# Attention of a streaming encoder layer: when the streams' loads are asked for, how many splits precede the first job, and in what rounds the value products run

## The reference, cut to what matters

```
z = rmsnorm(x) @ w_in                      # q_A k_A v_A forget_A q_B k_B v_B
A (8 heads x 64): softmax(q k^T / 8 + C[t] - C[s]), s <= t, C = cumsum(log sigmoid(f))
B (8 heads x 64): softmax(q k^T / 8 + rel_bias[t-s]), own chunk of 64 and the 8 before it
streams: the same, with 1024 cached keys (A) or 512 (B) before the 16 new ones
x += rmsnorm(concat(rmsnorm(o_A), rmsnorm(o_B)) @ w_out)
x += rmsnorm((silu(h @ w_gate) * (h @ w_up)) @ w_down)
```

## Time and profile before

| what | us |
|---|---|
| median of 3 runs (lowest, highest) | 3291.67 (3288.47, 3296.19) |
| the profiled execution's own time | 3288.23 |
| its span, first to last instruction | 3286.5 |
| TensorE busy over the span | 2942.9 (90%) |
| VectorE, ScalarE, GpSimd busy | 1659.4, 1208.5, 469.6 |

### The profile page before, as it was taken

How to read it: one execution, slowest core, us unless ns; L and a number is a source line. 1 busy time by engine, 2 the same in 40 slices (tenths; PEclk the granted TensorE clock), 3 DMA queues, 4 the chain that set the end, 5 groups by cost and what they waited for, 6 DMA issues and landing times. The chain is left out here.

```text
span 3286.5 us, 57063 instructions
## 1 busy us (share of the span) xinstructions
PE 2942.9 (90%) x23073; PEld 2633.0 (80%) x23073; DVE 1659.4 (50%) x3253; ACT 1208.5 (37%) x2124; POOL 469.6 (14%) x402
## 2 busy tenths in 40 slices
PE   7999999688888667787994999999999996998998
PEld 7999999577677445655884999999999994886887
DVE  6222221377666445664445766786676653223444
ACT  5320000266666344553443333433343333223211
POOL 0000000100000000000113544453344320000000
PEclk9999999899999789998996999999999998999999
DMA  5322121412211765434543322333222225434553
GB/s 166 89 78 76 63 72 60 137 39 76 74 36 46 211 201 181 145 112 167 162 141 118 141 104 103 122 107 105 105 87 105 105 79 164 106 93 135 176 176 118
DMA packets 275868, 376.37 MB, mean 115 GB/s; under 512 B 16456, under 2 KB 203864, under 8 KB 263576
## 3 DMA queue, kind: packets, MB, share of 16 engines
q1 hardware_dynamic: 273368, 368.43, 35.3%
q10 hardware_dynamic: 2240, 4.30, 0.4%
HBM read 283.52 MB, written 89.15 MB: 113 GB/s over the span
## 5 line engine op out<-in xcount | busy, mean ns | idle before, releaser
L2064 PE MATMUL dwn_py<-dwn_wh,dwn_ah 128*128 128x512 f32 x748 | 296.9, 397 | 42.0 <-DVE dwn_al L2139 32.6
L1117 ACT ACTIVATE att_pts<-att_pt 128x384 f32<-128x384 f32 (+3 forms) x444 | 207.7, 493 | 284.6 <-PE att_pt L999 255.6
L2065 PE MATMUL dwn_py<-dwn_wl,dwn_ah 128*128 128x512 f32 x748 | 294.1, 393 | 0.0
L2066 PE MATMUL dwn_py<-dwn_wh,dwn_al 128*128 128x512 f32 x748 | 293.9, 393 | 0.0
L1106 ACT ACTIVATE att_sx<-att_sx,att_nm 128x640 f32<-128x640 f32 (+17 forms) x272 | 265.2, 976 | 19.0 <-DVE att_os L1276 17.7
L1035 PE MATMUL att_po<-att_pts,att_vv 128*64 128x128 f32 x3296 | 230.0, 286 | 44.0 <-DVE att_os L1276 38.2
L1035 PEld LDWEIGHTS att_po<-att_pts,att_vv 128*64 128x64 f32 x3296 | 195.0, 144 | 66.2 <-issue 62.1
L999 PEld LDWEIGHTS att_pt<-att_eye,att_sx 64*128 64x128 f32 x3296 | 132.2, 141 | 130.8 <-ACT att_pts L1117 83.1
L79 PE MATMUL frt_pz<-frt_xhi,frt_hi 128*128 128x448 f32 (+1 forms) x640 | 230.5, 360 | 0.0
L81 PE MATMUL frt_pz<-frt_xhi,frt_lo 128*128 128x448 f32 (+1 forms) x640 | 230.5, 360 | 0.0
L80 PE MATMUL frt_pz<-frt_xlo,frt_hi 128*128 128x448 f32 (+1 forms) x640 | 230.1, 359 | 0.0
(11 more groups left out here) (251 smaller groups left out, 7473.7 us busy)
## 6 DMA issues: line engine op xcount, KB each, us to landing
gup_wr<-in_w_gu SPq DMA_DIRECT2D x65, 1024.0 KB, 5.1
dwn_ar<-mid_act SPq DMA_DIRECT2D x67, 704.0 KB, 6.0
att_raw<-out_zT SPq DMA_DIRECT2D x64, 256.0 KB, 3.0
att_bb<-in_cache_ak SPq DMA_DIRECT2D x16, 1024.0 KB, 8.3
att_bb<-in_cache_av SPq DMA_DIRECT2D x16, 1024.0 KB, 14.2
mid_act<-gup_ao SPq DMA_DIRECT2D x44, 362.0 KB, 2.5
out_zT<-frt_shared SPq DMA_DIRECT2D x64, 224.0 KB, 1.9
frt_raw<-in_w_slab SPq DMA_DIRECT2D x11, 1024.0 KB, 5.3
```

Of the source, the lines that this page charges most:

```text
L1117: nc.scalar.activation(pts[G % NPT][:, :, 0:k, 64 * x:64 * x + 64], pt[x][:].rearrange("p (e j q) -> p e j q", e=2, q=64)[:, :, 0:k, :], A ...
L2064: nc.tensor.matmul(out, ah[u][:, j, :], wh[:, j, :], start=(j == 0), stop=False)
L2065: nc.tensor.matmul(out, ah[u][:, j, :], wl[:, j, :], start=False, stop=False)
L2066: last = nc.tensor.matmul(out, al[u][:, j, :], wh[:, j, :], start=False, stop=(j == NJ - 1))
```

## The change

It has four parts, all in `attend`.

1. Splits. The slices are taken in the order k0, q0, k1, q1 and so on. Two are split ahead of job 0, and two more after each of the jobs 0, 1 and 2 (`first_splits`); the scores of pair 0 wait for two slices per four jobs. `stream_consts` moves behind the first copy of job 6, and its scratch tile moves.
2. Loads. `load_keys` no longer brings the table, and is issued one loop sooner (at 63 for stream 0, else one loop ahead of the present stream's). `load_table` is new: tables 0 and 1 at loop 64, the table of stream s+2 in the loop after stream s, behind the values of s+1.
3. Rounds. `value_order` sets them: two groups when three are held, one group when two of different jobs are held, else none. In two-group jobs each round is turn_out(n-1), values(n, 0), values(n, 1), ahead of turn(n+1, 1), at odd or even G alike.
4. VectorE's walk follows the same rounds.

```diff
+def value_order(order):
+    out, held = {}, []
+    for what, n, g in order:
+        if what == "turn":
+            first_ends = len(held) == 2 and held[0][0] != held[1][0]
+            k = 2 if len(held) == 3 else 1 if first_ends else 0
+            out[n, g] = held[:k]
+            held = held[k:] + [(n, g)]
+    out["rest"] = held
+    return out
...
+    CHUNKS = [0, 4, 1, 5, 2, 6, 3, 7]
...
-        own = sx[2][:, 0, 0:GW]
+        own = sx[2][:, 1, SEQ - GW:]
...
+        def first_splits(n):
+            return [2 * n + 2, 2 * n + 3] if n < 3 else []
...
+                    if n == WIDE - 1:
+                        load_keys(0)
                     if n == WIDE:
                         load_queries()
-                        load_keys(0)
+                        load_table(0)
+                        load_table(1)
                         load_values(0)
-                    if n in STREAM_AT and p + 1 < NST:
-                        load_keys(p + 1)
+                    if n + 1 in STREAM_AT and JOBS[n + 1][1] + 1 < NST:
+                        load_keys(JOBS[n + 1][1] + 1)
                     if n - 1 in STREAM_AT and JOBS[n - 1][1] + 1 < NST:
                         load_values(JOBS[n - 1][1] + 1)
+                        if JOBS[n - 1][1] + 2 < NST:
+                            load_table(JOBS[n - 1][1] + 2)
...
-                    if i == 0:
+                    if p == 0 and i % 4 == 0:
+                        pe.wait_ge(s_lo, 2 * (i // 4 + 1))
+                    if p > 0 and i == 0:
                         pe.wait_ge(s_lo, 8 * (p + 1))
...
-                        if (T0[n] + g) % 2 == 0:
+                        if VALUES[n, g]:
                             for x in ended:
                                 turn_out(x)
                             ended = []
-                            for x in held[:-1]:
+                            for x in VALUES[n, g]:
...
-                for x in range(8):
+                for x in range(2):
                     split_high(x)
...
-                            for x in splits_at(n):
+                            for x in first_splits(n) + splits_at(n):
                                 split_high(x)
...
-                stream_consts()
-                for x in range(8):
+                for x in range(2):
                     split_low(x)
...
+                        for y in first_splits(n):
+                            split_low(y)
+                        if (n, g) == (6, 0):
+                            stream_consts()
```

More of the change, by code:

```diff
@@ L645, in attend @@
     ORDER = attend_order()
+    VALUES = value_order(ORDER)
     CH = GW // P
@@ L749, in load_raw @@
                 def load_raw(x):
-                    p, c = divmod(x, 8)
+                    p, c = x // 8, CHUNKS[x % 8]
                     base, off = rows(p)
@@ L799, in load_keys, with load_table @@
                         sp.dma_start(kr[x % 2], keys[b][:, :, h * 512:(h + 1) * 512]).then_inc(l_k[x % 2], 16)
+                def load_table(s):
+                    band, b = divmod(s, NB)
                     if band == 0:
@@ L1054, in _ @@
                 pe.wait_ge(s_cst, 1)
-                held, ended = [], []
+                ended = []
                 for what, n, g in ORDER:
@@ L1067, in _ @@
                                     ended.append(x[0])
-                            held = held[-1:]
                         turn(n, g)
-                        held.append((n, g))
                 for x in ended:
@@ L1073, in _ @@
                 ended = []
-                for x in held:
+                for x in VALUES["rest"]:
                     values(*x)
```

## The result

The changed kernel takes 3206.59 us (median of 4 runs, 3203.83 to 3209.14) against 3293.02 (4 runs, 3288.47 to 3296.19): ratio 0.9738, 95% interval 0.9722 to 0.9755, 86 us gained. The forecast was 3225 with a range of 3202 to 3257. The sign and the range hold; the gain is 20 us larger than forecast. Its profiled execution took 3205.57 us, with a span of 3203.8.

A forecast was written before the change was run, and what follows sets the result against it. TensorE, busy for 90% of the span, was taken as the bound: time is its work plus waits. Start 4, loads 38, clock 9 and rounds 15 make 66 us off 3288.2: 3222, or 3225 as a median, range 3202 to 3257.

The forecast's parts named there:

- Start: Start of the stage: bias step 12 us sooner, splits between first jobs cost 7.6, job 4 turns 4 us sooner, bounds 0 to 12.
- Loads: Long streams: of 41.0 us of key and table waits 38 go, bounds 28 to 41; 9 us more from the clock.
- rival (b): Long streams: sooner keys delay the same loop's slice, ScalarE holds its copies, eight holds of 2 us; 3250 us, chance 0.08.
- The bound of 28: Low bound on the load waits won: half of the later waits return, as values, table and slice are queued in another order.
- The clock item: Long streams: less TensorE work at half clock behind the waits, 9 us won, bounds 0 to 17.
- Rounds: Value rounds: 52 us of eviction waits go, 30 return as waits for exps; 22 taken as 15 us, bounds -5 to 35.
- (a): Value rounds: they give nothing, as exps wait as long as evictions did; 3242 us, chance 0.15.
- (c): First turns of 96 fox or band jobs: the exp chain decides, each waits 1.2 us more; slower, 3303 us, chance 0.02.
- (d): Loads not really sooner, start bound by the bias load, only the rounds left; near no change, chance 0.03.
- two signs of being wrong: Key or slice waits staying above 10 us, or the sum of exps and copy waits growing by over 50.
- key and table waits under 4 us: Sign of being right: TensorE's waits for keys and tables come to under 4 us in all.
- job 4 at 641: Sign of being right at the start: job 4's first turn comes near 641 us on the timeline.

The follow-up runs named there:

- e1: The kernel before with the new rounds (parts 3 and 4) alone, loads and splits as before: 3230.11 us, ratio 0.9811.
- e7: The changed kernel with half of the queries and new keys asked for behind the values of stream 0: 3208.63 us, ratio 0.9737.
- e2: The kernel before with the loads asked for sooner (part 2) alone: 3263.66 us, ratio 0.9909.
- e9: The rounds alone as in e1, but SyncE held at some jobs behind the first band job until their last turn: 3230.32 us, ratio 0.9800.
- e4: The changed kernel with the old rounds, so new splits and loads only: 3264.81 us, ratio 0.9918.
- e3: The kernel before with the first splits (part 1) alone: 3297.41 us, ratio 1.001.
- e5: The changed kernel, but VectorE takes a copy's second half where no value products precede the next turn, instead of at even G: 3208.00 us, ratio 0.9733.
- e8: The changed kernel with the edits of e5, e6 and e7 together: 3196.29 us, ratio 0.9700.
- e12: The changed kernel with the edits of e8 and e11 together: 3198.22 us, ratio 0.9701.
- e6: The changed kernel, but in the loop behind a stream the slice is asked for ahead of values and table: 3198.63 us, ratio 0.9705.
- e10: e6 without the first splits, all eight slices of pair 0 split ahead of job 0 again: 3201.39 us, ratio 0.9713.
- e11: e6 with the slice asked for ahead of the keys too, in the loop before each stream's: 3194.19 us, ratio 0.9699.

## Why the prediction was right, and where it was off

**Start: 4 us, measured 3, of which 2.3 by the splits.** From the last product of the stage before to job 4's first turn 39.2 us became 36.2. The bias step came where it was put (621.76 for 622), and so did slice 3: asked for at 615.31, it let its split begin at 625.73, against 626.02 before. Being asked for sooner gained it nothing, as the order of the queue said. The forecast had 640.7 for job 4 and got 642.9: from the first bias step to there it took 21.1 us instead of 11.1 + 7.6, so the splits between the jobs cost 10.0 us instead of 7.6, since the copies, exps and scores behind them waited too (3.76, 1.29, 2.35 and 1.76 us on TensorE). Of the 3 us, 2.3 are the splits' (38.5 in e1, without them) and the rest the rounds'; the forecast's 4.3 had left the eviction wait out, so 2.3 is what it must be held against.

**Loads: 38 us of waits and 9 of clock, measured some 27 alone.** The waits themselves fell by 34 where 38 was said; the first table was under-sized (3 us left in the forecast, 6.6 measured; e7 doesn't say why). The failed step is that nothing was put down for the slices in the same queue. The text knew the mechanism and gave it to rival (b) with a chance of 0.08, at eight holds of 2 us. It happened: in e2 the copy waits grew by 20 us in four holds, in the changed kernel two holds took 5.3 and 6.9. The bound of 28 ("half of the later waits come back") is nearer in size, but not by its mechanism: the waits for keys did not come back, and what came were waits for copies. The clock item was of the right size: 9 us said, 8.6 among the long streams in e2 (188.98 to 180.40), 7.9 over the three stretches.

**Rounds: 15 us, measured 61 alone and 58 on top.** This is the term that was mis-sized, and beyond its bound of 35. Its first half held: 52.0 us of eviction waits went, and exps and copies came back with 26.5 for the 30 that 50 jobs at 0.6 us gave. The step that failed was the last one, which took 22 down to 15 because "an engine that no longer waits at one place arrives sooner at the next". The runs show the opposite: nothing was lost behind the evictions, and 15 us of key and table waits and 14 us of TensorE's own busy time went with them. The sum gave the rounds no share of either. Why the key and table waits fell stays open (e9). Of the 14 us, the 7.5 among the long streams have a counterpart in the 8.8 from e4 to the changed kernel; there the waits of 3 us and more went from 27.4 to 13.5 us with the rounds alone and from 30.0 to 18.8 on top of the loads. The prediction thus looked for the clock's price at the right place, behind the long waits, but not for an effect of the rounds on it. The 6.5 us among the short streams are not shown to be the rounds'. The 0.96 there, which the prediction read as the level that stays, was itself low: the other traces with the old rounds had 0.98 to 1.00.

**The sum** came out near by luck, because the two errors have opposite signs: the rounds gave 43 to 46 us more than said, the loads and their clock 20 to 26 less, the start 1 less; together they make about the 20 us by which 86 stands above 66.

**The rivals.** (a) The rounds give nothing: refuted by e1. (b) True as a mechanism, for about a tenth of what the change won, and removable. (c) Exps and copies waits grew by 37 us in all, under the 50 that was the mark. (d) Refuted: the first keys left 15 us ahead of their score. Of the signs named ahead, no wait for `att_os`, the clock over 0.93 and exps waits up by 15 to 30 (17) were met; "key and table waits under 4 us" was not (7.2), nor job 4 at 641 (642.9). Of the two signs of being wrong, one appeared: waits for slices above 10 us. ScalarE stood 24.1 us for slices between 1030 and 1320, hardly less than before (25.8), and two of these waits reached TensorE as holds of over 5 us.

## What to carry to other kernels

Sort a bound engine's waits by what ends them, and count a stretch's busy time at two clocks: here 65 eviction waits of 0.8 us on average went, and with them 15 us of waits elsewhere and part of the time that TensorE spent at the lower clock. When a large prefetch is moved ahead in a shared queue, look at which small load of the same queue some in-order engine waits for; putting the small one first won 8 us. A clock read from one trace of one kernel is not a level to build on; read the same stretch in several. And a forecast made of several terms can be right in the sum with each term wrong, so parts should be run one by one before any is believed.

## What was not expected of the hardware

The granted clock (a mean over its levels of 1.2 and 2.4 GHz) is lowest just behind TensorE's longer waits. In the changed kernel it was 0.72 in each of the stretches 1050 to 1062, 1086 to 1098 and 1182 to 1194, in which the waits of 6.6, 5.3 and 6.9 us end, and 1.00 in most of the other stretches of 12 us. The Trainium skill (TensorE: Matmul & The Clock Gate, HAM oscillation) describes this loss of clock behind waits for data, and these rows agree.

Over the whole stretch of the long streams the clock goes roughly with the waits of 3 us and more (a limit that I chose only for sorting). The kernel before and e3 have six and seven of them at 0.85; e1, e2, e4 and e9 three to five at 0.89 and 0.90; the changed kernel, e5, e7, e8 and e12 three at 0.94 and 0.95; e6 and e10 two at 0.95; e11 one at 0.98. This also separates e11 from e12, whose waits are nearly the same in all (42.2 and 40.1 us) but whose busy times differ by 5.5 us: one wait of 5.3 us against three of 4.9, 4.4 and 3.5. Each of these is one execution, and no run changed one such wait alone, so this is a pattern and not a shown price.

What I did not expect is the stretch of the short streams. Its longest wait is at most 2.4 us in every kernel with the old rounds, and the waits add up to 32.8, 32.1, 35.4 and 32.9 us in the kernel before, e2, e3 and e4. The clock was 0.96, 0.98, 0.99 and 1.00, and TensorE's busy time 136.9, 134.4, 132.9 and 131.0 us for the same products. With the new rounds it was 130.3 at 0.99 (e1) and 128.4 at 1.00 (changed kernel). So the clock of such a stretch moved by up to 0.04 and 6 us with no change in its waits. Differences of 5 us between single profiled executions can't be read as the worth of an edit.
